# A float32 hybrid decoder layer: x and its vectors as host-made columns, and the order of a seven-product pass changed

## What is computed

```
h    = rmsnorm(x, g_pre_mix)                 # x * rsqrt(mean(x*x) + 1e-6) * g
proj = h @ w_in                              # 2048 x 2560: q, k, v and the pooling input u
a    = sliding-window attention with sinks and ALiBi; pl = causal pooling mixer of u
x1   = x + rmsnorm(concat(a, pl) @ w_out, g_post_mix)
y    = x1 + rmsnorm(square(relu(rmsnorm(x1, g_pre_ffn) @ w_up)) @ w_down, g_post_ffn)
```

## Time and profile before

| | |
|---|---|
| runs before, median of 3 | 2049.05 us (2047.56 to 2049.23) |
| the profiled execution's own time | 2047.78 us |
| its span, first to last instruction | 2046.0 us |
| PE busy | 1973.5 us, 96% |
| DVE busy | 1272.8 us, 62% |
| ACT busy | 1236.2 us, 60% |
| POOL busy | 890.9 us, 44% |

### The profile page before, as it was taken

The page is one execution under the profiler, slowest core; times in us unless marked ns, Lnnn a source line. Parts: engine busy times, 40 slices in busy tenths (PEclk is TensorE's granted clock), DMA queues, the critical chain, the costliest instruction groups (busy, mean ns, idle before and its releaser), DMA issues.

```text
span 2046.0 us, 39225 instructions
## 1 busy us (share of the span) xinstructions
PE 1973.5 (96%) x15450; PEld 1941.7 (95%) x15450; DVE 1272.8 (62%) x1966; ACT 1236.2 (60%) x1823; POOL 890.9 (44%) x619
## 2 busy tenths in 40 slices
PE   7999999999988899999999999989999999999998
PEld 6999999899978899999999999989999999999998
DVE  3455543622258776676676676666666666666687
ACT  5234421422264466776776777767777777777784
POOL 0000022211125666766666666654544454444472
PEclk9999998999989899999999999999999999999999
DMA  5411121252233356556556556795656556565542
GB/s 172 165 62 61 55 73 57 77 175 84 92 127 118 122 176 205 170 185 203 174 182 202 177 181 200 228 318 182 213 191 207 181 180 204 185 213 191 182 158 89
DMA packets 271342, 328.16 MB, mean 160 GB/s; under 512 B 8192, under 2 KB 236936, under 8 KB 270063
## 3 DMA queue, kind: packets, MB, share of 16 engines
q1 hardware_dynamic: 267680, 315.66, 47.4%
q10 hardware_dynamic: 3479, 9.99, 1.3%
HBM read 253.79 MB, written 74.22 MB: 160 GB/s over the span
## 4 chain that ended last, share of the span: by engine, by line
PE 59%; DVE 4%; issue 2%; DMA 1%; POOL 1%; ACT 0%; DVEq 0%; SPq 0%; POOLq 0%; ACTq 0%
PE banks L2248 20%; PE banks L2250 19%; PE banks L2249 19%; DVE mlp_rows L1689 3%; DVE quads L1671 1%; DMA mlp_kept<-mlp_rows 1%; DMA mlp_part<-mlp_kept 1%; PE banks L2266 0%; DVE x_tok L1813 0%; ACT mlp_hi L1182 0%; DVE splits L1645 0%; POOL mlp_rows L871 0%; POOL mlp_rows L873 0%; ACT mlp_rows L1176 0%; ACT splits L1159 0%
## 5 line engine op out<-in xcount | busy, mean ns | idle before, releaser
L2248 PE MATMUL banks<-mlp_part,splits 128*128 128x272 f32 x1792 | 517.8, 289 | 6.0 <-DVE y_sum L1668 2.5
L2250 PE MATMUL banks<-mlp_part,splits 128*128 128x272 f32 x1792 | 517.0, 288 | 0.0
L2249 PE MATMUL banks<-mlp_part,splits 128*128 128x272 f32 x1792 | 516.1, 288 | 0.0
L2248 PEld LDWEIGHTS banks<-mlp_part,splits 128*128 128x128 f32 x1792 | 336.6, 188 | 7.4 <-ACT splits L1159 7.0
L2249 PEld LDWEIGHTS banks<-mlp_part,splits 128*128 128x128 f32 x1792 | 340.8, 190 | 0.0
L2250 PEld LDWEIGHTS banks<-mlp_part,splits 128*128 128x128 f32 x1792 | 336.6, 188 | 0.0
L1671 DVE TENSOR_TENSOR y_sum<-y_sum,banks 128x272 f32<-128x272 f32 x416 | 182.2, 438 | 187.7 <-PE banks L2250 187.6
L2248 PE MATMUL banks<-s_part,splits 128*128 128x272 f32 x960 | 279.1, 291 | 7.8 <-ACT splits L1159 3.2
L2250 PE MATMUL banks<-s_part,splits 128*128 128x272 f32 x960 | 278.4, 290 | 0.0
L2249 PE MATMUL banks<-s_part,splits 128*128 128x272 f32 x960 | 277.2, 289 | 0.0
L1857 PE MATMUL banks<-acts_hi,w_hi 128*128 128x272 f32 x1184 | 253.1, 295 | 9.4 <-DVE uT L1357 4.1
(11 more groups left out here) (265 smaller groups left out, 4429.2 us busy)
## 6 DMA issues: line engine op xcount, KB each, us to landing
raw_down<-in_w_down SPq DMA_DIRECT2D x128, 512.0 KB, 4.4
raw_up<-in_w_up SPq DMA_DIRECT2D x120, 512.0 KB, 7.8
mlp_part<-mlp_kept SPq DMA_DIRECT2D x56, 1088.0 KB, 8.3
mlp_kept<-mlp_hi SPq DMA_DIRECT2D x32, 952.0 KB, 4.5
mlp_kept<-mlp_rows SPq DMA_DIRECT2D x32, 952.0 KB, 5.7
w_raw<-in_w_in SPq DMA_DIRECT2D x40, 512.0 KB, 3.5
w_raw<-in_w_out SPq DMA_DIRECT2D x32, 512.0 KB, 3.4
x_kept<-x1T SPq DMA_DIRECT2D x8, 544.0 KB, 2.8
```

The source lines that it names most:

```text
L2248: nc.tensor.matmul(out, wh, xh, start=first, stop=False, skip_group_check=not STARTS[i])
L2249: nc.tensor.matmul(out, wh, xl, start=False, stop=False, skip_group_check=not STARTS[i])
L2250: ins = nc.tensor.matmul(out, wl, xh, start=False, stop=j == pairs - 1, skip_group_check=not STARTS[i])
```

## The change

1. The host lays out x as `x_cols` (features on partitions, all 544 rows behind each other) and the norm vectors with the pooling scale as `vec_cols`. The kernel loads them as columns: `x_raw`, in 8 pieces of two feature tiles between the first four weight units, and `vecs`. All turns of x in the first projection and those of the vectors go. `x_raw` lies where `acts_lo` is written, so the rest of a tile overwrites its input.
2. The sums of squares come from PE: ACT squares each tile into `sq_tmp`, which holds two tiles, and PE multiplies the squares with a column of ones (`first_sums`, five products of one column), tile by tile, into bank 7. DVE adds the 16 results. The spread of the scales moves from behind unit 3 to the middle of unit 4.
3. `HIGH_FROM = 0`: the PSUM copies serve all products of the up pass.
4. `mlp_low(G + 1)` moves from behind the take of product 3 to that of product 4; at the head of the up pass `mlp_low(0)`, the rests of the input sums, POOL's `activation_sums(0)` and ACT's `sum_high(3, 1)` change places.

```
-        HIGH_FROM = 2 * NP
+        HIGH_FROM = 0
...
+            def load_x(i):
+                sp.dma_start(x_raw[:, 2 * i:2 * i + 2, :], x_cols[:, 2 * i:2 * i + 2, :]).then_inc(x_landed[i], 16)
+
+            sp.dma_start(vecs[:], vec_cols).then_inc(vec_landed[0], 16)
             load_x(0)
...
             gp.wait_ge(h_summed, 4)
             t1(0)
             t3(0)
+            activation_sums(0)
             t2(0)
-            activation_sums(0)
...
+            act.wait_ge(vec_landed[0], 16)
             for kt in range(KT):
-                act.wait_ge(x_turned, kt + 1)
-                nc.scalar.activation(acts_hi[:, kt, :], flat(2 * x_slot(kt), T), ACT.Copy, scale=g_pre[:, kt:kt + 1]).then_inc(h_hi, 1)
+                act.wait_ge(x_landed[kt // 2], 16)
+                nc.scalar.activation(acts_hi[:, kt, :], x_raw[:, kt, :], ACT.Copy, scale=g_pre[:, kt:kt + 1]).then_inc(h_hi, 1)
+                if kt >= 2:
+                    act.wait_ge(x_summed, kt - 1)
+                nc.scalar.activation(sq_tmp[:, kt % 2 * T:(kt % 2 + 1) * T], x_raw[:, kt, :], ACT.Square).then_inc(squares, 1)
...
-            dve.wait_ge(pre_ready, 1)
+            dve.wait_ge(vec_landed[0], 16)
             for kt in range(KT):
                 dve.wait_ge(h_hi, kt + 1)
+                dve.wait_ge(squares, kt + 1)
...
             sum_low(2, KT + 1)
             low_part(0)
-            mlp_low(0)
+            sum_low(3, KT + 2)
             dve.wait_ge(sums_turned, 2)
             dve.wait_ge(unit_used, U_END)
             relu_plain(1, plain_rows)
             low_part(1)
-            sum_low(3, KT + 2)
             take(0)
+            mlp_low(0)
             low_part(2)
...
-                if i == 3:
+                if i == 4:
                     mlp_low(G + 1)
...
+            def first_sums(kt):
+                pe.wait_ge(squares, kt + 1)
+                for c in range(TOK):
+                    rows = tok_rows[c]
+                    at = kt % 2 * T + c * P
+                    ins = nc.tensor.matmul(banks[0:rows, 7, P + c * KT + kt:P + c * KT + kt + 1], sq_tmp[:, at:at + rows],
+                                           ones[:, 0:1], start=True, stop=True)
+                ins.then_inc(x_summed, 1)
+
+            def first_tiles(q):
                 for kk in range(UNIT_KT):
                     kt = q * UNIT_KT + kk
-                    pe.wait_ge(h_lo, rows + kt + 1)
+                    pe.wait_ge(h_lo, kt + 1)
                     for nt in range(2):
+                        ins = product(slot(nt), q % SPLIT_SLOTS, kk, nt, acts_hi[:, kt, :], acts_lo[:, kt, :], kt == 0, kt == KT - 1)
...
+                    if kt > 0:
+                        first_sums(kt - 1)
+                    if kt == KT - 1:
+                        first_sums(kt)
```

More of the change, by code:

```diff
@@ L151, in hybrid_decoder @@
         acts_lo = at("acts_lo", H_AT + KT * T * 4, [P, KT, T], F32R)
+        x_raw = at("x_raw", H_AT + KT * T * 4, [P, KT, T])
         w_raw = at("w_raw", R0_AT, [P, RAW_SLOTS, UNIT_KT * UNIT_N])
@@ L577, in _ @@
                     load(pair * K_UNITS + kq, 0, w_in_v[kq, :, :, n0:n0 + UNIT_N])
-                    if pair + kq == 0:
-                        load_x(1)
+                    if pair == 0:
+                        for i in ((1, 2), (3, 4), (5, 6), (7,))[kq]:
+                            load_x(i)
             for j in range(POOL_UNITS):
@@ L939, in _ @@
             take_root(0)
             split(4)
-            act.wait_ge(x_turned, KT)
-            act.wait_ge(squares, 2 * TOK)
+            act.wait_ge(squares, KT)
             act.dma_start(state_tok, state_pool[0].rearrange("b s c -> (b s) c")).then_inc(state_landed, 16)
-            rows = [(g_post_mix, 0, KT), (g_pre_ffn, KT, KT), (g_post_ffn, 2 * KT, KT), (pool_scale, 3 * KT, UT)]
-            for i, (vec, at, n) in enumerate(rows):
-                act.dma_start(vec_rows[at:at + n, :], vec[0].rearrange("(k p) -> k p", p=P)).then_inc(vec_landed[i + 1], 16)
@@ L1881, in pair_tiles @@
                         between(q, 1)
-            def tile_by_tile(u, pair, rows, q, half_way):
+            def first_sums(kt):
[6 more added lines that the diff above has]
+                ins.then_inc(x_summed, 1)
@@ L1915, in _ @@
-            for kt in range(UNIT_KT):
-                first_turn(kt)
+                    if kk == UNIT_KT - 1:
+                        ins.then_inc(unit_used, 1)
+                    if kt > 0:
+                        first_sums(kt - 1)
+                    if kt == KT - 1:
+                        first_sums(kt)
+            pe.wait_ge(consts, 6 + 2 * GQA + PAIRS)
             def turn_new_keys():
@@ L1941, in turn_vectors @@
                 pe.wait_ge(consts, 7 + 2 * GQA + PAIRS)
-                for i in range(1, 7):
+                for i in range(1, 3):
                     pe.wait_ge(vec_landed[i], 16)
                 pe.wait_ge(old_k_act, 2)
-                n = 3 * KT + UT
-                nc.tensor.transpose(banks[:, 4, 0:n], vec_rows, ident[0:n, 0:n])
                 nc.tensor.matmul(banks[:, 5, 0:HEADS], ones[0:1, 0:1].broadcast_to([1, P]), sink_row, start=True, stop=True)
@@ L2109, in _ @@
                 if pair == 0:
-                    tile_by_tile(j, 0, 0, q, mid)
-                    after(j)
+                    first_tiles(q)
                     continue
@@ L2303 @@
     depth, dec_b, window, kv_heads, hd = inputs['cache_k'].shape
+    d = inputs['x_prompt'].shape[-1]
+    x = np.concatenate([inputs['x_prompt'].reshape(-1, d), inputs['x_sample'].reshape(-1, d)])
+    x_cols = np.ascontiguousarray(x.T.reshape(d // P, P, -1).transpose(1, 0, 2))
+    vec = np.concatenate([inputs[name].reshape(-1) for name in ('g_pre_mix', 'g_post_mix', 'g_pre_ffn', 'g_post_ffn', 'pool_scale')])
+    vec_cols = np.ascontiguousarray(vec.reshape(-1, P).T)
+    for name, a in (('x_cols', x_cols), ('vec_cols', vec_cols)):
+        arrays[f"in_{name}"] = a
+        args.append(nc.dram_tensor(f"in_{name}", a.shape, mybir.dt.from_np(a.dtype), kind="ExternalInput").ap())
     _, _, state, pool_w = inputs['state_pool'].shape
```

97 lines of the change are left out of this document (21 added, 76 removed).

## The result

The changed kernel takes **2119.66 us** (median of four runs, 2119.01 to 2121.03) beside 2049.1 for the kernel before on the same chip: ratio 1.0345, 95% interval 1.0328 to 1.0361. That is 71 us slower. The profiled execution took 2119.03 us with a span of 2117.3, where the one before took 2047.78 with 2046.0; both medians are within 1.4 us of these.

The account below looks back on a forecast made before the run. PE, busy 96% of the span, was taken to bound the kernel. Start +46.5, head -3, steady up pass +10 and hand-over +1.5 made +55 on 2047.8, so 2103 us was forecast, range 2076 to 2126.

Parts of the forecast that it names:

- the start: First projection up to unit 5: +46.5 us, some +32 at a 4.2 us tile and +60 at 6.2.
- the later remainder with the hand-over: mlp_low one product later: +10 us in the steady up pass, plus +1.5 at the hand-over to the down pass.
- the head: Head of the up pass, reordered and with PSUM copies: -3 us, ends -9 and +4.
- The pass over 16 tiles: Start, x tiles: 5.2 us a tile, ends 4.2 and 6.2; unit 4 starts at 94.5 against 53.58, +41.
- The loop: Start: square waits for sums, rest for square, product for rest; a gap of 1.7 us a tile.
- the rival that the clock stays down: Start: clock low in the whole pass over x, tile 6.2 us, 14 us more, 2117; chance 0.12.
- the main case: Whole kernel: 5.2 us a tile in the start, 2103 us in all; chance 0.52.
- The row that spoke for a fast clock: Profile row cited for the clock staying up in the start: a PE wait of 1.60 us had not lowered it.
- Unit 5: Start: unit 5 about 13.7 us after unit 4, where it was 8.1; +5.5 us.
- Steady up pass: Up groups: relu waits for the later store's landing, +0.35 us a group, +10 in 28; ends -12 and +14.
- Hand-over: Up to down pass: store_lo of the last groups later by 1.8 us; +1.5 us, ends 0 and +2.
- The rival "faster" at 2035: Start: squares run a tile further ahead, tile 2.5 us, unit 4 at 55.2, sum -14; chance 0.04.

Follow-up runs that it names:

- e1: The changed kernel with a place of its own for the raw x tiles; 2077.75 us, ratio to before 1.0139.
- e2: The changed kernel with four square tiles in place of two; 2069.75 us, ratio to before 1.0100.
- e10: The changed kernel with six unused 272-column matmuls behind each of 14 groups of sums; 2106.56 us, ratio to before 1.0282.
- e7: The changed kernel with mlp_low still at the fifth product, but ahead of the rest of the next weights on DVE; 2138.22 us, ratio to before 1.0430.
- e3: The changed kernel with fourteen unused 272-column matmuls behind each of 14 groups of sums; 2094.02 us, ratio to before 1.0221.

## Why the prediction was right, and where its sizes were off

The forecast was 2103 in 2076 to 2126; the time is 2119.7. The mechanisms held in the main, and the sign. The sizes did not: the start was put at +46.5 and cost 62.1, the later remainder with the hand-over at +11.5 and cost 17.4, the head at -3 and gave 8.6. That is 21.5 us too little loss and 5.6 too little gain, so the time lies nearer to the forecast than its terms do, and in that there is luck.

- *The pass over 16 tiles.* The loop is as written, fifteen waits of DVE for the square, fourteen of ACT for the sums and fourteen of PE for the rest, with idle times of 1.63 to 1.73 us of PE against 1.7 forecast, and e1 and e2 show that each link is needed. What was mis-sized is the period: I took 5.2, "the middle, because at the low clock products fill nearly half of the time and may bring the clock back". It came back three times, each time for about half a tile (the product at 23.84 above begins with it); the granted clock was 0.56 and the period 6.13. The forecast's own ends were good: 4.2 at full clock (4.35 in e10, 4.34 in e7) and 6.2 at half (6.42 from 36.09 to 42.51, a tile with no fast part). 13 or 14 tiles at 0.93 more are 12 to 13 us of the 13.4 by which unit 4 came later than forecast. So what happened is the rival that the clock stays down, at 2117 with a chance of 0.12, and not the main case.
- *Why the clock was misjudged.* The row that spoke for a fast clock was an idle time of 1.60 us that had not lowered it. There PE did full-width products up to the gap and behind it; here each gap follows one-column sums. Whether that makes the difference no run separates. Even idle times of 0.68 (e10) and 1.11 us (e1) ahead of such a tile were followed at times by its loss, and 1.63 in e7 at first was not; without idle time it was kept (e2, e3). By the Trainium skill (TensorE: Matmul & The Clock Gate, HAM oscillation) the clock goes where PE idles longer between bursts than any of these gaps; the trace disagrees, at 0.56 over 80 us in which no idle time of PE is over 1.73.
- *Unit 5.* +5.5 was forecast, 61.2 - 54.3 = +6.9 came. The stall ahead of unit 4 that was forecast as 3.9 from DVE's first sum is there, 3.34 of idle PE.
- *Head.* -3 was forecast between -9 and +4; it gave 5.7 up to the first seven-product group, and 8.6 with what follows. "Product 3 then starts about where it did" was wrong: 6.29 us of wait for the second `relu_plain` became 0.60, and product 3, which now waits 3.38 us for DVE's rest where it waited 2.27, starts at 735.85, 14.6 us behind the first product of the group, where it was 13.6. `mlp_low(0)` behind `take(0)` took back 1 us and not all.
- *Steady up pass.* +0.35 a group was forecast, +0.57 came (22.4 against 21.83). The landing did become the bound, 51.5 us in 29 waits, and the 0.4 us waits for the take gave way to waits of about 1 us for the splits, as written. (The profile names ACT's high part for them; in the group above DVE's rest ends 0.28 us after it, at 987.83, and PE starts at 987.93.) The round was costed with the 2.13 us of `mlp_low` from its old place, and in the new one it takes 2.73 beside POOL: a duration that depends on its neighbour was carried over as a constant. These 0.60 us more were partly offset, since it starts 13.85 us behind `relu`, where 14.4 was reckoned; landing and hand-overs took 5.76 where 5.7 was reckoned.
- *Hand-over.* +1.5 forecast; PE's wait there went from 1.3 to 4.0 us, +2.7.
- *The rival "faster" at 2035* would have needed the squares to run ahead. e2 is that case: the tile is 2.64, near the 2.5 reckoned, and unit 4 starts at 58.1 (55.2). It is still slower than before once the later remainder is in.

## What to carry over

Before work is taken off a busy engine, follow one turn of the new loop through its buffers: a ring of two square tiles together with a place shared by two values made three half-idle engines take turns, and the cure was more buffer in either place (four square tiles, or a place of its own for x), not less work. A gap on TensorE can cost more than its length, as beside the one-column sums here; in a loop that idles, price both clock levels and do not take the middle. A step moved on VectorE changes its length with what GpSimd does beside it, and a store that was covered by 1.5 us of slack binds as soon as its issue moves by more.

## What the runs showed of the hardware that was not expected

- 196 matmuls without use made the kernel 26 us faster (e3), since they kept the clock at 1.00 instead of 0.56.
- In a stream of products and one-column sums the clock stayed at 1.00 after a first idle time of 1.11 us; after a second, 11.7 us later, came 18 us at a granted clock of 0.53, in which PE was busy for 98% (e1). The same stream without a gap stayed at 1.00 (e2). Why it took 18 us to come back there, and why the clock in e10 and e7 fell after some tiles and not after others with equal gaps, was not tried and stays open.
- Ten one-column sums take 1.03 us at full clock (e2, 28.80 to 29.83) and 1.82 at half (e1, 36.99 to 38.81) from their start to the next product's. That is the factor 1.8 by which 272-column matmuls differ too, 0.25 and 0.45 us a pair from start to start.
- A VectorE operation with two SBUF inputs and a GpSimd tensor operation do not slow each other by shares: in the three pairs above the one that began first runs at its usual length and the other waits, up to 2.1 us.
